# Two two-layer transformer blocks on one core: layers unrolled, weights packed as contiguous slabs, and the modulation matrices sent through the weight ring

## The chip, the cores and the metric

The kernel runs on one NeuronCore of a Trainium2 chip (trn2). The metric is the device time of one execution in microseconds (us); lower is better. Everything is float32.

## What is computed

The input x has 512 tokens of width 1024. It passes through two blocks of two layers each. A layer has a token mixer and a feed-forward part, and both are modulated by vectors that come from one conditioning vector c and a 1024 x 6144 matrix of the layer:

```
mod = silu(c) @ w_mod[l] + b_mod[l]                  # 6144 values, cut in six: sh1, sc1, g1, sh2, sc2, g2
h = _rms(x, ln1[l]) * (1 + sc1) + sh1
x = x + g1 * _mixing(h, ...)                         # w_in, three kinds of attention, w_o
h = _rms(x, ln2[l]) * (1 + sc2) + sh2
x = x + g2 * ((silu(h @ w_gate[l]) * (h @ w_up[l])) @ w_down[l])      # hidden width 2816
```

The second block has the same frame with its own matrices: its mixer has two kinds of attention and a state-space part, and its feed-forward part is `square(relu(h @ w_up)) @ w_down` with hidden width 4096. So there are four modulation matrices of 24 MB each (w_mod for two layers, w_ada_2 for two), which are used for one row only. The mod vector of a layer is needed when that layer starts.

## The kernel before

Activations lie transposed: xT and hT hold 1024 features as 8 tiles of 128 partitions x 512 tokens. Every large product takes 128 x 128 weights as the stationary operand and 512 tokens as the moving one, eight or more in a row into one bank (`gemm`, L775). One such float32 product is recorded as two MATMUL instructions, so "x32" in a row is 16 products.

Weights come in slabs of up to 2 MB (4096 words per partition) through a ring of two slots (`RING = 2`). SyncE issues the loads in a list's order (`SLABS1`, `SLABS2`, L607 and L664): slab n goes to slot n mod 2, and before its load SyncE waits until the last product that reads slab n-2 is done (`LAST1`, `LAST2`). In the feed-forward part of block 1 a slab `gu` holds two column tiles of w_gate and two of w_up and serves the steps gu 2s and 2s+1, 32 products; a slab `down` holds one column tile of w_down, 22 products. In block 2 a slab `up` serves four steps of 8 products, a slab `down` one step of 32.

The modulation matrices do not use the ring. They come as 24 pieces of 1 MB (256 columns each) into two stages that lie in the tiles SPT and sel. VectorE multiplies the eight row tiles of a piece by silu(c) and adds them (`mod_sum`, L1432 and L1434), and TensorE sums the result over the partitions with two products with a single moving column (`mod_product`, L783). For the first layer all 24 pieces are done before anything else (L588 to L596). For each following layer they are spread over the feed-forward part of the layer before (steps `ma` and `mm`), with loads issued behind the slabs. Block 2 runs its two layers as a loop over one program, so its second layer does this work as well, though no layer follows.

Each block is a hardware loop (`Fori`) over its two layers. The engines run hand-written lists of steps (`order1`, `order2`) in order; TensorE, ScalarE and VectorE each take their part of each step. A step takes banks of PSUM in turn from one of two groups of four, MAIN and SIDE. In the attention of block 1 there are 48 units (sc, nr, tp, pv), each with small products at L877, L883 and L893.

Small vectors (biases, gains, lambda) come from 40 or so small transfers issued by GpSimd; c and c_2 come from SyncE, one word per partition.

Of the kernel before, what the change touches and what calls it, by code (L numbers as in the profile page):

```python
# [42 lines left out]
RENEW = 100  # L43
# [55 lines left out]
def fresh(engine, value):  # L99

    r = engine.alloc_register()
    engine.reg_mov(r, value)
    return engine.snap(r, donate=True, min_val=0, max_val=DEPTH - 1)

class Signal:
# [8 lines left out]

    def after(self, l, k):
        return self.sem, l * self.per + (self.base + k)

    def check(self):
        assert self.seen == self.per, (self.sem, self.seen, self.per)  # L120
# [16 lines left out]
class Banks:  # L137

    def __init__(self, full, free, base):  # L140
        self.full, self.free, self.base = full, free, list(base)
        self.where, self.uses, self.turn = {}, [0] * 8, {}
# [8 lines left out]
    def bank(self, job):  # L151
        return self.where[job][0]

    def before(self, l, job):
        b, n = self.where[job]
        return self.free[b], l * self.uses[b] + (self.base[b] + n)

    def ready(self, l, job):
        b, n = self.where[job]
        return self.full[b], l * self.uses[b] + (self.base[b] + n + 1)  # L160

    def taken(self, l, job):

        b, n = self.where[job]
        return self.free[b], l * self.uses[b] + (self.base[b] + n + 1)

    def taken_before_second(self, l, job):
        b, n = self.where[job]
        return self.free[b], l * (n + 1) + self.base[b]

    def ready_before_second(self, l, job):

        b, n = self.where[job]
        return self.full[b], l * (n + 1) + self.base[b]

    def after_layers(self):
        return [self.base[b] + DEPTH * self.uses[b] for b in range(8)]
# [24 lines left out]
def order1():  # L202
    o = [("prep",), ("norm", 0)]
# [41 lines left out]
    for u in range(n + 3):  # L245
        if u < n:
            o.append(("sc", u))
        if 0 <= u - 1 < n:
            o.append(("nr", u - 1))
        if 0 <= u - 2 < n:  # L250
            o.append(("tp", u - 2))
        if 0 <= u - 3 < n:
            o.append(("pv", u - 3))
    for t in range(8 + 1):
# [5 lines left out]
    o.append(("norm", 1))  # L260
# [12 lines left out]
STEPS1 = order1()  # L273

SLABS1 = ([("qi", 0, 5), ("v", 0, 4), ("qaqb", 0, 2), ("kbkc", 0, 5), ("qc", 0, 1)]
          + [("wo", s, 1) for s in range(2)] + [("gu", s, 2) for s in range(FT1 // 2)] + [("down", s, 1) for s in range(KT)])
assert len(SLABS1) % RING == 0 and DEPTH == 2

# [4 lines left out]
LAST1.update({("down", s): ("down", s) for s in range(KT)})  # L283

def plan_banks(steps, jobs_of, full, free, base):
    b = Banks(full, free, base)
    for st in steps:
        for job, group in jobs_of(st):
            b.add(job, group)  # L290
    return b

def jobs1(st):
# [5 lines left out]
    if kind in ("norm", "pss", "rope", "idx", "bz", "br", "sc", "tp", "on"):  # L300
        return [(st, SIDE)]
    if st == ("mm", 0):
        return [(("mod",), SIDE)]
# [7 lines left out]
V2_N = W_LAM + 128  # L311

# [13 lines left out]
def order2():  # L326
    o = [("prep",), ("norm", 0)]
# [29 lines left out]
    for w, last in ((0, "wo"), (1, "down")):  # L357
# [6 lines left out]
        if w == 0:  # L364
            o.append(("norm", 1))
# [9 lines left out]
STEPS2 = order2()  # L375
SLABS2 = ([("cq", 0, 1), ("v", 0, 2), ("mix", 0, 3), ("xbc", 0, 1), ("z", 0, 1),
                                                ("aqk", 0, 1)]
          + [("wo", s, 1) for s in range(2)] + [("up", s, 1) for s in range(FT2 // 4)]
          + [("down", s, 1) for s in range(KT)])
assert len(SLABS2) % RING == 0  # L380
# [4 lines left out]
LAST2.update({("down", s): ("down", s) for s in range(KT)})  # L385

def jobs2(st):
# [9 lines left out]
    if st == ("mm", 0):  # L398
        return [(("mod",), SIDE)]
    if kind in ("norm", "cqss", "kvss", "kr", "mqr", "dtt", "tp", "an", "xd", "G", "da", "sn"):  # L400
        return [(st, SIDE)]
# [3 lines left out]
def pieces_behind(slabs, first, each):  # L405

    out, p = {}, 0
    names = [k[:2] for k in slabs]
    for n in range(names.index((first, 0)) + 1, len(names)):
        out[names[n]] = list(range(p, min(p + each, PIECES)))  # L410
        p = min(p + each, PIECES)
    assert p == PIECES
    return out

BEHIND1 = pieces_behind(SLABS1, "gu", 2)
BEHIND2 = pieces_behind(SLABS2, "up", 3)

class Slabs:  # L420

    def __init__(self, slabs, landed, base):
        self.slabs, self.landed, self.base = slabs, landed, list(base)
        self.per = [0] * RING
        self.at = {}
        for n, (kind, s, dmas) in enumerate(slabs):
            self.per[n % RING] += 16 * dmas
            self.at[(kind, s)] = (n, n % RING, self.per[n % RING])

    def slot(self, key):
        return self.at[key][1]

    def ready(self, l, key):
        n, slot, count = self.at[key]
        return self.landed[slot], l * self.per[slot] + (self.base[slot] + count)

    def after_layers(self):
        return [self.base[s] + DEPTH * self.per[s] for s in range(RING)]

def build(nc, A, out, blocks=(1, 2)):
    ctx = ExitStack()
    with ctx:
# [3 lines left out]
        def sem(name):  # L448
# [19 lines left out]
        modN = sb("modN", [P, 6 * KT])  # L468
        modT = sb("modT", [P, 6 * KT])
        bias4 = sb("bias4", [P, LAYERS, 6 * KT])  # L470
        biasN = sb("biasN", [P, 6 * KT])
        cN = sb("cN", [P, KT])
# [3 lines left out]
        cT = sb("cT", [P, 2, KT])  # L476
        csc = sb("csc", [P, 2, KT])
        vec = sb("vec", [P, V2_N])
        vall2 = sb("vall2", [P, DEPTH, V2_N])
        vall1 = sb("vall1", [P, DEPTH, 36])  # L480
# [10 lines left out]
        stage = [SPT[:, 0:4, :].rearrange("p (k a) n -> p k (a n)", k=1).rearrange("p o (k n) -> p (o k) n", k=KT),  # L491
                 sel[:, :, :].rearrange("p (k a) n -> p k (a n)", k=1).rearrange("p o (k n) -> p (o k) n", k=KT)]
        acc = [SPT[:, 4, 0:PIECE], SPT[:, 5, 0:PIECE]]
# [18 lines left out]
        cst_in = sem("cst_in")  # L512
# [21 lines left out]
        macc = sem("mod_summed")  # L534
        mread = sem("mod_read")
        mland = [sem("mod_landed0"), sem("mod_landed1")]
        mod_in = sem("mod_bias_in")
        ma1, ma2 = Signal(macc, PIECES, PIECES), Signal(macc, PIECES, PIECES * (1 + (DEPTH if 1 in blocks else 0)))
        mr1 = Signal(mread, PIECES - 1, PIECES - 1)
        mr2 = Signal(mread, PIECES - 1, (PIECES - 1) * (1 + (DEPTH if 1 in blocks else 0)))  # L540
        ml1 = [Signal(s, 8 * PIECES, 8 * PIECES) for s in mland]
        ml2 = [Signal(s, 8 * PIECES, 8 * PIECES * (1 + (DEPTH if 1 in blocks else 0))) for s in mland]
        base0 = [2] + [1] * 7
        bk1 = plan_banks(STEPS1, jobs1, full, free, base0)
        sl1 = Slabs(SLABS1, landed, [0] * RING)
        block = ctx.enter_context(nc.Block())
        do1, do2 = 1 in blocks, 2 in blocks
        base1 = bk1.after_layers() if do1 else base0
        bk2 = plan_banks(STEPS2, jobs2, full, free, base1)
        sl2 = Slabs(SLABS2, landed, sl1.after_layers() if do1 else [0] * RING)  # L550
# [12 lines left out]
        final = bk2.after_layers() if do2 else base1  # L563
# [6 lines left out]
        V_LN1, V_LN2, V_QNA, V_KNA, V_QNC, V_KNC, V_SINK, V_GOUT, V1_N = 0, 8, 16, 17, 18, 19, 20, 28, 36  # L570
        vec_in = sem("vec_in")
        vec2_in, pos_in = sem("vec2_in"), sem("pos_in")
        VEC_DMAS2 = DEPTH * 14
        VEC_DMAS1 = DEPTH * (3 + 8 + 1)
# [3 lines left out]
        def _(sp):  # L578
            sp.dma_start(cst[:, :], A["consts"]).then_inc(cst_in, 16)
# [3 lines left out]
            with nc.allow_non_contiguous_dma(reason="c lies one word per partition"):  # L583
                sp.dma_start(cT[:, 0, :], A["c"][0].rearrange("(t p) -> p t", p=P)).then_inc(x_in, 16)
                sp.dma_start(cT[:, 1, :], A["c_2"][0].rearrange("(t p) -> p t", p=P)).then_inc(x_in, 16)

            def load(sl, l, n, dst, src):
# [1316 lines left out]
```

## Time and profile before

| | |
|---|---|
| median of 3 runs | 3943.94 us (3939.78 to 3944.48) |
| span of the profiled execution | 3928.9 us |
| TensorE busy | 3512.1 us, 89% of the span, in 8996 instructions |
| VectorE busy | 1441.1 us, 37% |
| ScalarE busy | 644.8 us, 16% |
| bytes moved | 329.77 MB, mean 84 GB/s |

The profile is one execution. Its span runs from the first to the last instruction, 15 us less than the median of the timed runs. A line such as L775 is the place in the kernel's text that issued the instruction.
### The profile page before, as it was taken

To read this page: it belongs to the slowest core of one execution; us is meant where nothing else is said; L and a number is where in the kernel's file an instruction comes from. 1 tells how busy PE (TensorE), PEld (TensorE's weight loads), DVE (VectorE), ACT (ScalarE), POOL (GpSimd) and SP (SyncE) were. 2 spreads that over 40 slices of the span, in tenths; PEclk is the share of its full clock that TensorE was granted. 3 is DMA by queue.
4 is the path that set the end of the run, shared out by engine and by line. 5 is a ranking of instruction groups with operands and counts; after the bars stand their busy time and mean duration, and the time that the engine had idled before them with its cause. 6 is when DMAs were issued, how large, how long until landed. Compare 5 with 4: busy or idle time off the path is not lost.

```text
span 3928.9 us, 27849 instructions
## 1 busy us (share of the span) xinstructions
PE 3512.1 (89%) x8996; PEld 1631.5 (42%) x8996; DVE 1441.1 (37%) x3459; ACT 644.8 (16%) x1425; POOL 45.5 (1%) x61
## 2 busy tenths in 40 slices
PE   1497889999999698999997997999997998899997
PEld 1243444444444353444443443444443444344443
DVE  4548651333116854233201365344101337144101
ACT  0112441000011333100002242200001133200000
POOL 4000000000000000000000000000000000000000
PEclk6698659999999756999998977999998978999999
DMA  8621002544332000344421200255231210145331
GB/s 167 179 65 43 1 1 64 164 136 148 84 77 65 22 1 1 107 145 155 130 74 46 86 22 0 78 186 172 78 77 38 82 43 1 64 161 171 99 83 43
DMA packets 363107, 329.77 MB, mean 84 GB/s; under 512 B 31265, under 2 KB 328737, under 8 KB 362833
## 3 DMA queue, kind: packets, MB, share of 16 engines
q1 hardware_dynamic: 360656, 327.48, 27.4%
q0 software_dynamic: 2304, 0.43, 0.5%
q8 instruction: 80, 1.31, 0.1%
q14 instruction: 67, 0.54, 0.1%
HBM read 325.79 MB, written 2.10 MB: 83 GB/s over the span
## 4 chain that ended last, share of the span: by engine, by line
PE 77%; DVE 12%; DMA 6%; issue 2%; ACT 2%; SPq 1%; DVEq 0%; ACTq 0%
PE bank L775 60%; DMA sel<-in_w_mods 5%; PE bank L877 3%; PE bank L893 2%; DVE SPT L1434 2%; DMA SPT<-in_w_mods 2%; PE bank L883 1%; DVE SPT L1825 1%; PE bank L1044 1%; PE bank L858 1%; DVE sel L1535 1%; PE bank L1028 1%; PE bank L783 1%; PE bank L812 1%; DVE m L1534 1%
## 5 line engine op out<-in xcount | busy, mean ns | idle before, releaser
L775 PE MATMUL bank<-hT,ring 128*128 128x512 f32 x4032 | 1785.6, 601 | 46.7 <-DVE hT L1457 15.5
L775 PEld LDWEIGHTS bank<-hT,ring 128*128 128x128 f32 x4032 | 764.8, 192 | 994.2 <-issue 984.6
L775 PE MATMUL bank<-U,ring 128*128 128x512 f32 (+1 forms) x1760 | 760.3, 593 | 3.3 <-DVE U L1861 2.3
L775 PEld LDWEIGHTS bank<-U,ring 128*128 128x128 f32 (+1 forms) x1760 | 332.6, 190 | 421.3 <-issue 421.3
L783 PE MATMUL bank<-cst,SPT 128*128 128x1 f32 x480 | 74.3, 259 | 135.4 <-DVE SPT L1434 135.4
L1625 DVE TENSOR_TENSOR U<-U,bank 128x512 f32<-128x512 f32 x44 | 30.3, 688 | 426.6 <-PE bank L775 426.6
L1854 DVE SCALAR_TENSOR_TENSOR hT<-hT,modG,rb 128x512 f32<-128x512 f32 x16 | 11.9, 746 | 456.7 <-ACT rb L1273 456.7
L1618 DVE SCALAR_TENSOR_TENSOR xT<-bank,modT,xT 128x512 f32<-128x512 f32 x32 | 24.0, 750 | 376.5 <-PE bank L775 376.5
L783 PEld LDWEIGHTS bank<-cst,SPT 128*128 128x128 f32 x480 | 79.5, 218 | 188.4 <-DVE SPT L1434 142.2
L1434 DVE SCALAR_TENSOR_TENSOR SPT<-sel,c,SPT 128x256 f32<-128x256 f32 x252 | 122.2, 485 | 9.0
L1434 DVE SCALAR_TENSOR_TENSOR SPT<-SPT,c 128x256 f32<-128x256 f32 x252 | 122.2, 485 | 9.0
L1861 DVE TENSOR_TENSOR U<-U 128x512 f32<-128x512 f32 x64 | 44.2, 691 | 208.7 <-ACT U L1406 208.7
L1239 ACT ACTIVATE U<-bank 128x512 f32<-128x512 f32 x44 | 26.3, 597 | 575.1 <-PE bank L775 575.1
L1265 ACT ACTIVATE sqb<-bank 128x512 f32<-128x512 f32 x38 | 22.7, 597 | 581.7 <-PE bank L775 568.4
L877 PE MATMUL bank<-U 64*128 64x256 f32 (+3 forms) x192 | 112.9, 694 | 0.0
L1406 ACT ACTIVATE U<-bank 128x512 f32<-128x512 f32 x64 | 38.2, 597 | 446.8 <-PE bank L775 446.8
L893 PE MATMUL bank<-SPT,VT 128*64 128x128 f32 x384 | 101.0, 414 | 0.0
L1434 DVE SCALAR_TENSOR_TENSOR SPT<-sel,cN,SPT 128x256 f32<-128x256 f32 x168 | 81.5, 485 | 6.0
L1434 DVE SCALAR_TENSOR_TENSOR SPT<-SPT,cN 128x256 f32<-128x256 f32 x168 | 81.5, 485 | 6.0
L1148 ACT ACTIVATE hT<-xT 128x512 f32<-128x512 f32 x32 | 17.8, 619 | 395.0 <-DVE xT L1618 152.9
L947 PE MATMUL bank<-hT,cst 128*128 128x512 f32 x64 | 39.9, 774 | 43.3 <-ACT hT L1294 43.3
L775 PE MATMUL bank<-ring,hT 128*128 128x452 f32 (+1 forms) x256 | 77.9, 465 | 0.0
(237 smaller groups left out, 2731.9 us busy)
## 6 DMA issues: line engine op xcount, KB each, us to landing
SPT<-in_w_mods SPq DMA_DIRECT2D x60, 1024.0 KB, 10.0
sel<-in_w_mods SPq DMA_DIRECT2D x60, 1024.0 KB, 9.7
ring<-in_w_up SPq DMA_DIRECT2D x16, 2048.0 KB, 8.1
ring<-in_w_down SPq DMA_DIRECT2D x16, 2048.0 KB, 9.1
ring<-in_w_gate SPq DMA_DIRECT2D x22, 1024.0 KB, 5.4
ring<-in_w_up SPq DMA_DIRECT2D x22, 1024.0 KB, 7.9
ring<-in_w_down SPq DMA_DIRECT2D x16, 1408.0 KB, 7.0
ring<-in_w_in SPq DMA_DIRECT2D x8, 2048.0 KB, 7.8
```

The lines of the kernel that those rows point to most:

```text
L775: mm = pe.matmul(dst, lhs(k), rhs(k), start=(k == 0), stop=(k == n - 1))
L783: mm = pe.matmul(bank[b][:, c:c + 1], acc[p % 2][:, P * j:P * j + P], ones[:, 0:1], start=True, stop=True)
L812: mm = pe.matmul(dst[:, :], ones, hT[:, k, :], start=(k == 0), stop=(k == KT - 1))
L858: mm = pe.matmul(dst[:, P * j:SEQ], w, SP[:, h % 2, j, P * j:SEQ], start=(j == kt), stop=(j == QT - 1))
L877: pe.matmul(dst[:, 0:P * len(ks)], PT[p, q, P * i:P * i + P], PT[p, k, P * ks[0]:P * ks[-1] + P], start=True, stop=True).then_inc(*done)
L883: mm = pe.transpose(dst[:, P * j:P * j + P], S[:, u % 3, P * j:P * j + P], ident)
L893: mm = pe.matmul(dst[p, 0:P], VT[:, kb, v:v + HD], pT[:, u % 3, P * j:P * j + P], start=(j == 0), stop=(j == len(ks) - 1))
L947: mm = pe.matmul(dst[:, :], ones, hT[:, k, :], start=(k == 0), stop=(k == KT - 1))
L1028: pe.matmul(bank[b][:, 0:n], U[p, A_Q + h // 2, P * i:P * i + P], U[p, A_K + h // 2, 0:n], start=True, stop=True, tile_position=(r, 0)).th ...
L1044: mm = pe.matmul(dst[p, 0:P], VT[:, j, v:v + HD], pT[:, u % 3, P * j:P * j + P], start=(j == 0), stop=(j == i))
L1434: ins = dve.scalar_tensor_tensor(a, w[:, k, :], c[:, k:k + 1], a, ALU.mult, ALU.add)
L1861: dve.tensor_tensor(U[:, f, :], U[:, f, :], U[:, f, :], ALU.mult).then_inc(*s2["u"].up())
```

## The change

The layers are unrolled: the loops `Fori` go, each layer has its own list of steps, and waits are on constants. All weights, the modulation matrices too, are packed on the host into one array of slabs, each laid out as the ring wants it (per partition one contiguous run of up to 16 KB), and each slab is one transfer. The order of the loads is the order in which the steps first use the slabs, over all layers and kinds (`ALL_SLABS`); `RING` stays 2. Small vectors are packed into one array as well, and the constants come in two transfers.

The modulation work changes its form. A matrix is 12 slabs of 2 MB (512 columns). TensorE multiplies a slab with silu(c) as the stationary operand: `cz` holds it as 32 columns of which one is not zero, and the eight row tiles of the slab are moving operands of 512 columns, sent to four column tiles of the array in turn (`mod_gemv`, tile position 0, 32, 64 or 96). ScalarE copies the bank to sqb, and four products with one moving column sum it and turn it into columns (`mod_turn`). VectorE adds the bias. The steps are mg and mp (mg2 and mp2 for the matrix of the next layer).

For the first layer only slabs 0 to 3 (shift and scale of the mixer, 2048 values) are done at the start; slabs 4 to 11 are done inside its attention, one in five units. The matrix of the next layer is done in the feed-forward part: in block 1 slab s right behind step gu 2s+1 (the last one behind down 0), in the first layer of block 2 slab p right behind step up 2p+1. The last layer of block 2 has none. The step norm is split into ns (squares, sum, product with the root) and nh (scale and shift).

```diff
-RENEW = 100
+MOD_SLABS = 6 * D // 512
+MOD_FIRST = 4
...
-def order1():
-    o = [("prep",), ("norm", 0)]
+def order1(l):
+    if l == 0:
+        o = [("ns", 0), ("mg", 0)]
+        for s in range(1, MOD_FIRST):
+            o += [("mg", s), ("mp", s - 1)]
+        o += [("mp", MOD_FIRST - 1), ("prep",), ("nh", 0)]
+    else:
+        o = [("prep",), ("ns", 0), ("nh", 0)]
...
+        if l == 0 and u % 5 == 0 and MOD_FIRST + u // 5 < MOD_SLABS:
+            o.append(("mg", MOD_FIRST + u // 5))
+        if l == 0 and u % 5 == 3 and MOD_FIRST + u // 5 < MOD_SLABS:
+            o.append(("mp", MOD_FIRST + u // 5))
...
     for f in range(FT1):
-        o += [("gu", f), ("ma", f)] + ([("mm", f - 1)] if f else [])
+        o.append(("gu", f))
+        if f % 2 and f // 2 < MOD_SLABS:
+            o += [("mg2", f // 2)] + ([("mp2", f // 2 - 1)] if f > 1 else [])
     for n in range(KT):
         o.append(("down", n))
-        if n < 2:
-            o += [("ma", FT1 + n), ("mm", FT1 + n - 1)]
-        if n == 2:
-            o += [("mm", PIECES - 1), ("mb",)]
+        if n == 0:
+            o += [("mg2", FT1 // 2), ("mp2", FT1 // 2 - 1)]
+        if n == 1:
+            o.append(("mp2", MOD_SLABS - 1))
...
             for f in range(FT2):
                 o.append(("up", f))
-                if f % 4 < 3:
-                    p = 3 * (f // 4) + f % 4
-                    o += [("ma", p)] + ([("mm", p - 1)] if p else [])
-            o += [("mm", PIECES - 1), ("mb",)]
+                if f % 2 and l < DEPTH - 1 and f // 2 <= MOD_SLABS:
+                    p = f // 2
+                    o += ([("mg2", p)] if p < MOD_SLABS else []) + ([("mp2", p - 1)] if p else [])
...
+for _blk, _layers, _of in ((1, STEPS1, slab_of1), (2, STEPS2, slab_of2)):
+    for _l, _steps in enumerate(_layers):
+        for _st in _steps:
+            _key = _of(_st)
+            if _key is not None and (_blk, _l) + _key not in ALL_SLABS:
+                ALL_SLABS.append((_blk, _l) + _key)
...
+            sp.dma_start(small[:, :], A["small"]).then_inc(small_in, 16)
+            sp.dma_start(cst[:, 0:2 * P], A["consts"][:, 0:2 * P]).then_inc(ident_in, 16)
...
+            for n, (blk, l, kind, s) in enumerate(ALL_SLABS):
+                if n >= RING:
+                    b0, l0, k0, s0 = ALL_SLABS[n - RING]
+                    sp.wait_ge(*(bk1 if b0 == 1 else bk2).ready(l0, (LAST1 if b0 == 1 else LAST2)[(k0, s0)]))
+                w = WIDTHS[(blk, kind)]
+                sp.dma_start(ring[:, n % RING, 0:w], A["slabs"][n, :, 0:w]).then_inc(landed[n % RING], 16)
+                if n == RING - 1:
+                    sp.dma_start(cst[:, 2 * P:C_N], A["consts"][:, 2 * P:C_N]).then_inc(cst_in, 16)
...
+            def mod_gemv(dst, m, key, sl):
+
+                pe.wait_ge(*sl.ready(l, key))
+                w8 = ring[:, sl.slot(l, key), :].rearrange("p (k n) -> p k n", k=KT)
+                for k in range(KT):
+                    r = 32 * (k % 4)
+                    mm = pe.matmul(dst[r:r + 32, :], cz[:, m, k, :], w8[:, k, :], start=(k < 4), stop=(k >= 4),
+                                   tile_position=(0, r))
+                return mm
...
+            def mod_turn(dst, s):
+
+                for j in range(4):
+                    mm = pe.matmul(dst[:, j:j + 1], sqb[:, s % 2, P * j:P * j + P], ones[:, 0:1], start=True, stop=True)
+                return mm
+
+            pe.wait_ge(cz_ready, 1)
+            pe.wait_ge(cst_in, 16)
...
+                    elif kind == "mg2":
+                        s = st[1]
+                        act.wait_ge(*bk1.ready(l, st))
+                        if s >= 2:
+                            act.wait_ge(*bk1.ready(l, ("mp2", s - 2)))
+                        act.activation(sqb[:, s % 2, :], src[:, :], ACT.Copy).then_inc(mod_row2, 1)
+                        act.wait_ge(mod_row2, MOD_SLABS * l + s + 1)
+                        act.sem_inc(*freed)
```

## Rows read from the trace of the kernel before

**Rows 1.** The page: busy time of each engine.

```profile
PE 3512.1 (89%) x8996; PEld 1631.5 (42%) x8996; DVE 1441.1 (37%) x3459; ACT 644.8 (16%) x1425; POOL 45.5 (1%) x61
```

**Rows 2.** Windows by stage: length, busy of PE, PEld, DVE, ACT, POOL, granted clock, DMA share, GB/s.

```profile
0.00:166.00 166.00, 29.58 (x128) 27.34 (x128) 98.52 (x208) 3.46 (x5) 45.51 (x61) 0.60 0.79 193
410.00:559.80 149.80, 142.54 (x422) 76.76 (x422) 81.12 (x350) 54.97 (x193) 0.00 (x0) 0.58 0.00 1
659.70:973.50 313.80, 313.31 (x788) 143.74 (x788) 95.25 (x197) 21.75 (x32) 0.00 (x0) 0.99 0.43 135
973.50:1126.00 152.50, 152.47 (x364) 68.33 (x365) 16.24 (x32) 4.41 (x7) 0.00 (x0) 1.00 0.36 94
2522.60:2772.70 250.10, 237.46 (x608) 109.58 (x608) 113.25 (x231) 23.93 (x39) 0.00 (x0) 0.98 0.46 151
3429.00:3674.70 245.70, 233.64 (x608) 107.80 (x606) 112.78 (x230) 23.39 (x39) 0.00 (x0) 0.99 0.47 154
```

**Rows 3.** Timeline of SyncE (SPq) and TensorE around one gu slab's end.

```profile
717.67 0.37 SPq L588 DMA_DIRECT2D ring<-in_w_gate  x1
...
703.45 13.98 PE L775 MATMUL bank<-hT,ring 128*128 128x512 f32 x32
717.63 13.98 PE L775 MATMUL bank<-hT,ring 128*128 128x512 f32 x32
```

**Rows 4.** DMA issues (count, KB, median us to landing), and GB/s per us from 310.

```profile
GB/s 0 20 240 408 403 412 391 223 0 0 0 0 0 8 0 0 0 0 0 0 0 0 0 0 0 0 0 0 0 0 0 0 0 0 0 0 25 178 371 403
ring<-in_w_o SPq DMA_DIRECT2D x2, 2048.0 KB, 7.8
...
ring<-in_w_down SPq DMA_DIRECT2D x16, 1408.0 KB, 7.0
cst<-in_consts SPq DMA_DIRECT2D x1, 2248.0 KB, 10.2
```

**Rows 5.** TensorE timeline: products on 32 columns; one 64-row product; two 32-row tiles; clock.

```profile
2139.05 7.05 PE L775 MATMUL bank<-hT,ring 128*32 128x512 f32 x16
...
474.30 1.22 PE L877 MATMUL bank<-U 64*128 64x256 f32 x2
...
2289.13 1.22 PE L1028 MATMUL bank<-U 32*128 32x256 f32 x4
...
470.00:480.00 10.00, 10.00 (x31) 5.41 (x31) 5.79 (x27) 3.90 (x16) 0.00 (x0) 0.50 0.01 2
2285.00:2295.00 10.00, 8.90 (x32) 4.04 (x28) 8.14 (x36) 4.16 (x18) 0.00 (x0) 0.50 0.00 0
```

**Rows 6.** TensorE timeline around short pauses (in brackets the idle time and its releaser).

```profile
2689.88 0.61 PE L783 MATMUL bank<-cst,SPT 128*128 128x1 f32 x4 [2.56 <-DVE SPT L1434]
2690.34 8.81 PE L775 MATMUL bank<-hT,ring 128*128 128x512 f32 x16
...
2713.53 7.11 PE L775 MATMUL bank<-hT,ring 128*128 128x512 f32 x16
...
2753.95 10.02 PE L775 MATMUL bank<-hT,ring 128*128 128x512 f32 x16
```

**Rows 7.** Windows of 1 us after TensorE idle times of 3.1 us, columns as in rows 2.

```profile
661.00:662.00 1.00, 1.00 (x2) 0.34 (x1) 1.00 (x3) 1.00 (x2) 0.00 (x0) 0.50 1.10 347
1137.00:1138.00 1.00, 1.00 (x4) 0.42 (x3) 1.00 (x2) 1.00 (x2) 0.00 (x0) 1.00 0.00 0
```

**Rows 8.** Timeline of the first 180 us: TensorE and ScalarE.

```profile
22.45 5.28 PE L766 MATMUL bank<-cst,U 128*128 128x128 f32 x32 [22.45 <-DMA cT<-in_c]
34.46 0.98 PE L783 MATMUL bank<-cst,SPT 128*128 128x1 f32 x4 [6.73 <-DVE SPT L1434]
166.00 8.65 PE L812 MATMUL bank<-hT,cst 128*128 128x512 f32 x16 [1.03 <-ACT hT L1148]
176.80 5.75 ACT L1157 ACTIVATE hT<-hT,modT,modA 128x512 f32<-128x512 f32 x8 [0.76 <-DVE hT L1497]
177.76 8.82 PE L775 MATMUL bank<-hT,ring 128*128 128x512 f32 x20 [3.11 <-ACT hT L1157]
```

More of the change, by code:

```diff
@@ L114, in up, with now, check @@
         return self.sem, 1
+    def now(self):
+        return self.sem, self.base + self.seen
     def after(self, l, k):
         return self.sem, l * self.per + (self.base + k)
-    def check(self):
-        assert self.seen == self.per, (self.sem, self.seen, self.per)
+    def check(self, times):
+        assert self.seen == times * self.per, (self.sem, self.seen, self.per)
 class Chain:
@@ L140, in __init__ @@
     def __init__(self, full, free, base):
-        self.full, self.free, self.base = full, free, list(base)
-        self.where, self.uses, self.turn = {}, [0] * 8, {}
+        self.full, self.free, self.uses = full, free, list(base)
+        self.where, self.turn = {}, {}
     def add(self, job, group):
@@ L283, with plan_banks @@
 LAST1.update({("down", s): ("down", s) for s in range(KT)})
-def plan_banks(steps, jobs_of, full, free, base):
+LAST1.update({("mod", s): ("mg", s) for s in range(MOD_SLABS)})
+LAST1.update({("mod2", s): ("mg2", s) for s in range(MOD_SLABS)})
+def plan_banks(layers, jobs_of, full, free, base):
     b = Banks(full, free, base)
-    for st in steps:
-        for job, group in jobs_of(st):
-            b.add(job, group)
+    for l, steps in enumerate(layers):
+        for st in steps:
+            for job, group in jobs_of(st):
+                b.add((l,) + job, group)
     return b
@@ L397, in jobs2 @@
         return [(("post", st[1]), SIDE)] if st[2] == 0 else []
-    if st == ("mm", 0):
-        return [(("mod",), SIDE)]
-    if kind in ("norm", "cqss", "kvss", "kr", "mqr", "dtt", "tp", "an", "xd", "G", "da", "sn"):
+    if kind in ("mg2", "mp2", "ns", "cqss", "kvss", "kr", "mqr", "dtt", "tp", "an", "xd", "G", "da", "sn"):
         return [(st, SIDE)]
     return []
[L405 to L413, printed above, removed]
@@ L443, in build @@
+def build(nc, A, out):
     ctx = ExitStack()
@@ L533, in build @@
         )
[L534 to L545, printed above, removed]
+        mod_row2 = sem("mod_row2")
+        bk1 = plan_banks(STEPS1, jobs1, full, free, [1] * 8)
+        sl1, sl2 = Slabs(1, landed), Slabs(2, landed)
         block = ctx.enter_context(nc.Block())
[L547 to L550, printed above, removed]
+        bk2 = plan_banks(STEPS2, jobs2, full, free, bk1.uses)
         s2 = dict(
@@ L581, in _ @@
             sp.dma_start(U[:, 0:8, :].rearrange("p (t a) n -> p t (a n)", t=QT),
                          A["x"][0].rearrange("(t p) d -> p t d", p=P)).then_inc(x_in, 16)
[L583 to L587, printed above, removed]
-                sp.dma_start(dst, src).then_inc(landed[n % RING], 16)
@@ L1105, in _ @@
-            if do2:
-                pe.wait_ge(*s2["x"].after(DEPTH - 1, 2 * KT))
-            else:
-                for n in range(KT):
-                    pe.wait_ge(*bk1.taken(DEPTH - 1, ("down", n)))
+            def mod_gemv(dst, m, key, sl):
[6 more added lines that the diff above has]
+                return mm
@@ L1452, in normed @@
                 if s1["pn"].seen:
-                    dve.wait_ge(*s1["pn"].after(l, s1["pn"].seen))
+                    dve.wait_ge(*s1["pn"].now())
                 link(dve.tensor_tensor(a, rb[:, k % 2, :], rb[:, k % 2, :], ALU.mult))
```

2379 lines of the change are left out of this document (1151 added, 1228 removed).

## The prediction

> **What bounds the kernel now.** I read the page first: TensorE is busy 89% of the span, VectorE 37% [rows 1]. The table by stage shows where that average hides two kinds of time [rows 2]. In the feed-forward stages TensorE has no holes: 313.3 of 313.8 us with the granted clock at 0.99 (gu, block 1) and 152.5 of 152.5 (down). In the first 166 us it does 29.6 us of work, while the first modulation matrix comes in and VectorE adds it up. The attention of block 1 is TensorE too, 142.5 of 149.8 us, but at a clock of 0.58.
>
> Then I looked at what the ring does when a slab is used up [rows 3]. The step pair that starts at 703.45 ends near 717.6; SyncE issues the next load at 717.67; TensorE starts the next 32 products at 717.63. It waits for nothing, since the other slot already holds the next slab. The load has a whole slab's time (28.3 us) to land. A 2 MB load lands 7.8 us after its issue and moves 390 to 412 GB/s while it runs; a down slab takes 7.0 us [rows 4].
>
> So two things decide: the 166 us at the start, which the change shortens, and the cover of the ring's loads.
>
> **The change part by part.** One product of 128 rows with 512 columns is 0.865 us (32 instructions, 13.84 of the 14.18 us from 703.45 to 717.63 [rows 3]); the other 0.34 us are the two small products of a modulation piece.
>
> *Cost of one modulation slab on TensorE.* Eight products with 32 stationary columns. Alone such a product costs what a full one does: 8 in 6.98 us [rows 5]. No row shows column tiles together. The nearest are row tiles: at a clock of 0.50 two products on different 32-row tiles (four instructions) take 1.22 us, as one 64-row product of the same 256 columns does (two instructions) [rows 5]. So disjoint tiles ran at the same time, in float32. The bounds are two rounds, 1.73 us, and no overlap, 6.9 us. I take the low end with some overhang, 2.0 us (3.8 at a clock of 0.50), because the row tiles overlapped fully. The turn (four small products) is twice a piece's: 0.7 us, or 1.9 at half clock (0.98 for two in [rows 8]).
>
> The Trainium skill speaks against this choice: "TensorE: Matmul & The Clock Gate", Part 3, says that weight loads overlap running matmuls only when the row group differs, and all four column tiles use the same rows; its measured speedup for three column tiles is 2.38. No trace of this kernel shows it. By full serialization the sum is the second rival below.
>
> *Start.* Now the first projection begins at 177.76 [rows 8]. After: the constants, which everything waits for, are the sixth transfer; 9.0 MB at 390 GB/s plus some 3 us give 26. The transposes (5.3 us) are covered by that. Squares and the sum over partitions: 1.1 + 8.65 us [rows 8], to 36. Slabs 0 and 1: to 41. SyncE can load slab 2 only when slab 0 is read (38.5), so it lands at 46.5, slab 3 near 49; with products and turns partly at half clock these end near 60. Preparation and the first scaled tile: 62. The qi slab, issued when slab 2 is read (about 50), has landed by 58. Gain 116 us. The 40 GpSimd transfers and the c loads vanish inside this.
>
> *Eight slabs in the attention of the first layer.* TensorE is the bound there, so all of it adds: 8 x (3.8 + 1.9) = 46 us at that clock [rows 2, 5]. ScalarE's copies (0.6 us each) lie beside it.
>
> *Feed-forward of block 1, two layers.* This is the large term. The list is now gu 0, mod 0, gu 1, mod 1 and so on, and the ring still has two slots: all gu slabs share one slot, all mod slabs the other. Slab gu s+1 may be loaded only when gu s is finished, exactly when TensorE wants it. What TensorE has meanwhile is one slab product and one turn, 2.7 us. The gap is the load: 0.1 + 7.8 + 0.1 = 8.0 us, ten times; then down 0 and down 1, same reason (22-product slabs, 6.1 us if their rate rises to that of 2 KB rows, 7.0 at most [rows 4]). From down 2 on the ring is doubled again. Away go 24 x 0.34 = 8.2 us. Idle for some 5 us, TensorE is likely to be slowed: after 2.56 us of idle and one small product the next eight products took 8.81 instead of 7.11 us, another time 10.02 [rows 6]; after 3.1 us the clock fell once and once not [rows 7]. I take 1.9 us for each of twelve. Sum per layer: 80 + 12.2 + 22.8 - 8.2 = 107; twice 214 us. VectorE's sums go, but it was no bound (95 of 313.8 us [rows 2]).
>
> *Up stage, first layer of block 2.* Here each up slab has two mod slabs behind it. The odd one takes the slot that the up slab leaves, and the next up slab is issued right after it: 4.2 MB at 400 GB/s, landing 7.9 and about 12.9 us after the last product. TensorE waits 7.9, multiplies cold and turns (5.7), so 13.6, plus 1.9 for the clock; the even slab adds 2.7. That is 18.2, six times: 109 us. The stage now takes 250.1 us for 32 groups of 6.92 = 222 [rows 2]; these pieces' 27 us go. Net 82.
>
> *Up stage, last layer.* No modulation work: 245.7 falls to about 225. Gain 21.
>
> *Unrolling and contiguous slabs.* The products follow each other at 0.4325 us per instruction in the loops already, so I cost the loop at nothing; in the attention of block 1, TensorE's idle 7.3 of 149.8 us [rows 2] bounds what leaner waits could gain in such a stage, and longer code fetches could cost as much. Contiguity gains nothing where 2 KB rows reach 400 GB/s [rows 4]; the constants (17.6 KB rows) took 10.2 us for 2.2 MB with other transfers in the queues. That bounds a slab at 9.3 us, and the sum at +45 for 30 exposed loads. The skill's "DMA: Bandwidth & Descriptors", Specifications, gives about 358 GB/s as a core's share of HBM; the measured 412 says otherwise, and by the page each load would be 0.7 us longer, 21 us in all.
>
> Sum: -116 + 46 + 214 + 82 - 21 = +205 on a span of 3928.9, so 4134. The median of the runs stands 15 us above the span: **4149 us**.
>
> **The rivals.** *A. Column tiles do not overlap.* Then a slab is 6.9 us (up to 13.7 at half clock). In block 1's feed-forward the load hides it (6.9 + 0.7 against 8.0), and with only 0.4 us idle the clock stays: 2 x (92.2 - 8.2) = 168. Start -98, attention about 93, up stage 6 x (7.9 + 10 + 1.2 + 7.6) - 27 = 133, last -21: +275, 4219 us.
>
> *B. The clock stays up.* No penalty after the gaps, and slabs in the attention at 2.7 us each: start -116, 22, 168, up stage 6 x (12.9 + 2.7) - 27 = 67, last -21: +120, 4064. For it speaks the second of [rows 7], against it a clock of 0.58 in the attention.
>
> *C. The loads are covered after all: faster.* If the next gu or up slab were there when the turn ends, each place would cost only the 2.7 us of TensorE: -116 + 46 + 2 x (32 - 8) + (32 - 27) - 21 = -38, 3906 us. It decides by one number: on average over the 30 places the slab must land within 1.3 us (38 / 30) after the turn, or 4.0 us after the last product of the slab before. At 7.8 us per load this needs twice the rate seen, or a third slot. The change text has two.
>
> *D. The matrices gain nothing at the start,* because constants and four slabs come late: proj at 100 instead of 62. Then 4187, inside the range.
>
> **How the numbers follow.** Forecast 0.55, A 0.20, B 0.13, D 0.06, C 0.05, rest 0.01. The range holds B at 4064 and A at 4219, with a little outside for a load of 7.3 or 9.3 us: 4050 to 4235. A measurement of this kernel can tell 0.2%, 8 us, from no change. Faster 0.05 (C), same 0.01, slower 0.94.
>
> **What would show each step.** In the trace after: projections begin near 62 us; mg2 groups of 16 instructions take about 2 us (A: 7); before each gu and down 0 and 1 TensorE waits 5 us for the DMA of the ring, 20 + 4 times, and twice per up slab in the first layer of block 2; SyncE issues a gu load at the end of the slab before and it lands 7.8 us later; the granted clock is 0.50 behind these waits; the last up stage takes 225 us. The forecast is wrong if the waits before gu are under 2 us (C), or if TensorE's own time for the slabs is three times mine (A).

## The result, and the profile after

The changed kernel takes 4077.27 us (median of 4 runs, 4059.55 to 4083.53) against 3941.86 us for the kernel before (4 runs, 3937.27 to 3944.48). The ratio is 1.034, 95% interval 1.032 to 1.037: slower, as forecast, inside the range, and 72 us below the predicted 4149. The profiled execution of after has a span of 4078.3 us, 149.4 more than that of before.

The page of after answers [rows 1 and 4]. In order: busy time of each engine, packets, the chain that ended last (shares by engine), the three groups that wait for the ring (L622 is `gemm`, L631 `mod_gemv`; busy, mean ns, idle before and its releaser), and the loads with their time to landing.

```profile
PE 3630.3 (89%) x9668; PEld 1645.8 (40%) x9668; DVE 999.9 (25%) x2538; ACT 673.9 (17%) x1473; POOL 1.7 (0%) x6
...
DMA packets 22952, 304.37 MB, mean 75 GB/s; under 512 B 2464, under 2 KB 2592, under 8 KB 3760
...
PE 81%; DVE 8%; DMA 7%; issue 3%; ACT 2%; DVEq 0%; SPq 0%; ACTq 0%
...
L622 PE MATMUL bank<-hT,ring 128*128 128x512 f32 x4032 | 1817.0, 612 | 150.8 <-DMA ring<-in_slabs 107.1
...
L622 PE MATMUL bank<-U,ring 128*128 128x512 f32 (+1 forms) x1760 | 768.5, 598 | 18.0 <-DMA ring<-in_slabs 15.1
...
L631 PE MATMUL bank<-ring,cz 128*32 128x512 f32 x768 | 110.8, 703 | 52.6 <-DMA ring<-in_slabs 52.6
...
ring<-in_slabs SPq DMA_DIRECT2D x124, 2048.0 KB, 7.8
ring<-in_slabs SPq DMA_DIRECT2D x16, 1408.0 KB, 6.2
```

TensorE is as busy as before in share, 89%, and does 118 us more. VectorE lost 441 us and GpSimd 44. What that work had cost TensorE before lay at the start and in short pauses of block 2's up stages (2.56 us in [rows 6]). New is the DMA of the ring in the chain: TensorE stands idle for it 107 us in front of gu slabs and the first projection, 15 us in front of down slabs and 53 us in front of modulation slabs. The packets fell from 363,107 to 22,952, and a 2 MB load lands in 7.8 us, as the loads with rows of 2 KB did before [rows 4].

The same stages as in [rows 2], in the columns of that table:

```profile
0.00:61.04 61.04, 29.60 (x145) 16.30 (x145) 12.76 (x31) 14.18 (x22) 1.71 (x6) 0.81 0.68 267
316.30:450.00 133.70, 129.78 (x566) 67.58 (x566) 68.91 (x327) 52.67 (x184) 0.00 (x0) 0.73 0.35 126
548.78:927.00 378.22, 326.64 (x874) 142.41 (x875) 18.39 (x35) 24.00 (x38) 0.00 (x0) 0.91 0.28 109
927.00:1124.61 197.61, 189.76 (x472) 84.12 (x471) 7.12 (x12) 9.36 (x13) 0.00 (x0) 0.97 0.23 84
2620.58:2943.23 322.65, 273.62 (x801) 118.45 (x801) 27.23 (x50) 31.08 (x51) 0.00 (x0) 0.90 0.33 125
3601.24:3824.37 223.13, 221.67 (x512) 97.74 (x513) 25.40 (x38) 23.91 (x39) 0.00 (x0) 0.99 0.19 67
```

The window of the attention (316.30 to 450.00) is narrower than the one in [rows 2]. From the starts of the stages in both timelines comes the balance of the span:

| stage | before | after | difference | forecast |
|---|---|---|---|---|
| start, to the first projection | 177.8 | 61.0 | -116.7 | -116 |
| block 1, layer 1: projections and attention, to w_o | 413.5 | 418.6 | +5.2 | +46 |
| block 1, layer 1: feed-forward (gu and down) | 466.4 | 575.8 | +109.5 | +107 |
| block 1, layer 2: feed-forward (gu and down) | 466.5 | 572.9 | +106.4 | +107 |
| block 2, layer 1: up | 250.1 | 322.7 | +72.5 | +82 |
| block 2, layer 2: up | 246.2 | 223.1 | -23.1 | -21 |
| all else (six pieces between -10.2 and +2.6) | | | -4.4 | 0 |
| span | 3928.9 | 4078.3 | +149.4 | +205 |

**The gu stage.** TensorE and SyncE's queue (SPq) in after, answering [rows 3]; the number in brackets is the idle time before the group.

```profile
691.74 1.92 PE L631 MATMUL bank<-ring,cz 128*32 128x512 f32 x16
691.84 39.86 SPq L592 DMA_DIRECT2D ring<-in_slabs  x4
693.60 1.05 PE L638 MATMUL bank<-cst,sqb 128*128 128x1 f32 x8
699.77 29.69 PE L622 MATMUL bank<-hT,ring 128*128 128x512 f32 x64 [5.12 <-DMA ring<-in_slabs]
```

The last product on slab gu 3 ends at 691.74, SyncE issues the load of gu 4 at 691.84, and the product that needs it starts at 699.77. Between them TensorE has one modulation slab (1.92 us) and one turn (1.05), and waits 5.12 us. Then the 64 instructions take 29.69 us, where the undisturbed stage needs 27.7: the granted clock behind the first of these waits is 0.50 for some 5 us (the window below) and then 1.00 (592 to 616). From the start of one slab's products to the start of the next it is 37.75 us (662.02 to 699.77) against 28.36 before: +9.4, where the forecast's terms give 8.0 + 1.9 - 0.7 = 9.2.

```profile
586.00:591.00 5.00, 4.90 (x6) 2.18 (x7) 0.00 (x0) 0.00 (x0) 0.00 (x0) 0.50 0.78 331
```

**The up stage** of block 2's first layer, the second and the first half of two up slabs:

```profile
2746.96 3.64 PE L631 MATMUL bank<-ring,cz 128*32 128x512 f32 x16 [7.90 <-DMA ring<-in_slabs]
2750.53 1.87 PE L638 MATMUL bank<-cst,sqb 128*128 128x1 f32 x8
2752.26 15.42 PE L622 MATMUL bank<-hT,ring 128*128 128x512 f32 x32
```

Here the modulation slab itself is late by the whole load, 7.9 us, and is then multiplied at half clock. There are six such waits, 7.7 to 8.0 us each.

**The attention of block 1.** Eight slabs were put into a stage in which TensorE hardly rests, and the stage grew by only 5 us. The windows say why: 316.3 to 450 ran at a granted clock of 0.73, while nearly the same part of it, the 48 units with their small products, had 0.52 before:

```profile
430.00:559.00 129.00, 126.12 (x361) 66.68 (x360) 68.93 (x318) 46.66 (x175) 0.00 (x0) 0.52 0.00 1
```

Around one slab, TensorE's timeline in after, and the windows over it:

```profile
339.35 1.22 PE L728 MATMUL bank<-U 64*128 64x256 f32 x2
...
341.74 3.64 PE L631 MATMUL bank<-ring,cz 128*32 128x512 f32 x16
345.31 0.71 PE L728 MATMUL bank<-U 64*128 64x256 f32 x2
...
350.28 1.05 PE L638 MATMUL bank<-cst,sqb 128*128 128x1 f32 x8
...
353.31 1.22 PE L728 MATMUL bank<-U 64*128 64x256 f32 x2
```

```profile
341.74:345.30 3.56, 3.56 (x17) 0.59 (x16) 0.65 (x2) 0.82 (x4) 0.00 (x0) 0.50 0.00 0
345.30:350.30 5.00, 4.85 (x29) 2.75 (x25) 3.59 (x18) 2.71 (x9) 0.00 (x0) 0.99 0.78 262
...
353.30:356.10 2.80, 2.80 (x9) 1.50 (x8) 1.74 (x8) 1.29 (x7) 0.00 (x0) 0.50 0.00 0
```

The score product of a unit takes 1.22 us ahead of the slab (clock 0.50), 0.71 behind it (0.99), and 1.22 again some 8 us later. By this reading the slab pays for itself with the faster units behind it. That is the theory which the experiments had to test, beside those on the feed-forward part.

The second layer of block 1 has no slabs in its attention and is a control for the unrolling. The same stretch in before and in after:

```profile
1400.00:1540.00 140.00, 132.70 (x370) 67.73 (x369) 75.08 (x296) 57.61 (x176) 0.00 (x0) 0.54 0.00 1
```

```profile
1400.00:1540.00 140.00, 133.26 (x373) 68.61 (x371) 74.24 (x300) 57.14 (x178) 0.00 (x0) 0.54 0.00 1
```

The clock is 0.54 in both, and projections plus attention take 414.0 us before and 416.5 after. So neither the unrolled program nor the contiguous slabs raised the clock or shortened this stage.

### The profile page after: what moved, and what is told of

It is laid out like the page before. It is cut to its first block, busy times and chain, and to the rows that moved or that the text cites. A ratio compares the mean times of both kernels' runs of the same rounds, so it can differ in the third digit from the quotient of the medians.

```text
span 4078.3 us, 25590 instructions
## 1 busy us (share of the span) xinstructions
PE 3630.3 (89%) x9668; PEld 1645.8 (40%) x9668; DVE 999.9 (25%) x2538; ACT 673.9 (17%) x1473; POOL 1.7 (0%) x6
## 2 busy tenths in 40 slices
DMA packets 22952, 304.37 MB, mean 75 GB/s; under 512 B 2464, under 2 KB 2592, under 8 KB 3760
## 4 chain that ended last, share of the span: by engine, by line
PE 81%; DVE 8%; DMA 7%; issue 3%; ACT 2%; DVEq 0%; SPq 0%; ACTq 0%
PE bank L622 64%; DMA ring<-in_slabs 6%; PE bank L728 2%; PE bank L744 2%; PE bank L631 1%; PE bank L734 1%; DVE SPT L1678 1%; PE bank L894 1%; PE bank L709 1%; DVE sel L1394 1%; PE bank L878 1%; PE bank L663 1%; DVE m L1393 1%; PE bank L937 1%; PE bank L885 1%
## 5 line engine op out<-in xcount | busy, mean ns | idle before, releaser
L622 PE MATMUL bank<-hT,ring 128*128 128x512 f32 x4032 | 1817.0, 612 | 150.8 <-DMA ring<-in_slabs 107.1
L622 PEld LDWEIGHTS bank<-hT,ring 128*128 128x128 f32 x4032 | 786.3, 196 | 1153.6 <-issue 1143.4
L622 PE MATMUL bank<-U,ring 128*128 128x512 f32 (+1 forms) x1760 | 768.5, 598 | 18.0 <-DMA ring<-in_slabs 15.1
L622 PEld LDWEIGHTS bank<-U,ring 128*128 128x128 f32 (+1 forms) x1760 | 336.0, 191 | 444.0 <-issue 444.0
L631 PE MATMUL bank<-ring,cz 128*32 128x512 f32 x768 | 110.8, 703 | 52.6 <-DMA ring<-in_slabs 52.6
L728 PE MATMUL bank<-U 64*128 64x256 f32 (+3 forms) x192 | 99.1, 615 | 0.0
L622 PE MATMUL bank<-ring,hT 128*128 128x452 f32 (+1 forms) x256 | 77.9, 465 | 0.0
L920 PE MATMUL bank<-SPT,sel 128*64 128x512 f32 (+3 forms) x128 | 59.0, 603 | 16.9 <-DVE SPT L1680 16.8
L1076 ACT ACTIVATE SPT<-SPT,st 128x256 f32<-128x256 f32 (+3 forms) x96 | 48.8, 508 | 146.8 <-DVE st L1446 83.8
L631 PEld LDWEIGHTS bank<-ring,cz 128*32 128x32 f32 x768 | 22.9, 121 | 120.6 <-issue 120.5
L744 PEld LDWEIGHTS bank<-SPT,VT 128*64 128x64 f32 x384 | 57.9, 189 | 24.8 <-issue 23.7
L689 PE MATMUL bank<-U,cst 128*128 128x512 f32 x48 | 29.1, 691 | 43.2 <-DVE U L1306 43.2
L638 PEld LDWEIGHTS bank<-cst,sqb 128*128 128x128 f32 x384 | 51.2, 207 | 39.0 <-issue 39.0
```

The source lines that it names most:

```text
L622: mm = pe.matmul(dst, lhs(k), rhs(k), start=(k == 0), stop=(k == n - 1))
L631: mm = pe.matmul(dst[r:r + 32, :], cz[:, m, k, :], w8[:, k, :], start=(k < 4), stop=(k >= 4), tile_position=(0, r))
L638: mm = pe.matmul(dst[:, j:j + 1], sqb[:, s % 2, P * j:P * j + P], ones[:, 0:1], start=True, stop=True)
L728: pe.matmul(dst[:, 0:P * len(ks)], PT[p, q, P * i:P * i + P], PT[p, k, P * ks[0]:P * ks[-1] + P], start=True, stop=True).then_inc(*done)
L744: mm = pe.matmul(dst[p, 0:P], VT[:, kb, v:v + HD], pT[:, u % 3, P * j:P * j + P], start=(j == 0), stop=(j == len(ks) - 1))
L920: mm = pe.matmul(dst[p, P * s:SEQ], sel[:, s, HD * h:HD * h + HD], mixing(4 * h + s)[:, P * s:SEQ], start=(s == 0), stop=(s == QT - 1))
```

## The experiments

All are edits of the changed kernel. The first four ran on one chip with the kernel before at 3932.41 us (7 runs, 3930.83 to 3950.69), the fifth with 3934.17 (9 runs, 3926.85 to 3939.69).

**1. The modulation slabs leave the ring.** The slabs of the next layer's matrix land in SPT and sel, which are idle in the feed-forward part, half in each, issued behind the weight slabs. The ring then alternates over weight slabs alone, as before the change (`RINGED` is ALL_SLABS without them). TensorE's work and all else stay.

```diff
-            for n, (blk, l, kind, s) in enumerate(ALL_SLABS):
+            for n, (blk, l, kind, s) in enumerate(RINGED):
...
+                for key in BEHIND.get((blk, l, kind, s), ()):
...
+                        sp.wait_ge(*bk.ready(l, ("mg2", key[3] - 1)))
...
+                    src = A["slabs"][ALL_SLABS.index(key)]
+                    sp.dma_start(SPT[:, 0:4, :].rearrange("p k n -> p (k n)"), src[:, 0:SLAB // 2]).then_inc(staged, 16)
+                    sp.dma_start(sel[:, :, :].rearrange("p k n -> p (k n)"), src[:, SLAB // 2:SLAB]).then_inc(staged, 16)
```

> The changed kernel with one difference: the slabs of the next layer's modulation matrix (mg2) do not pass through the weight ring but land in SPT and sel, half a slab in each, which lie idle in the feed-forward stage; products, column tiles and turns are the same. Theory 1 (the ring's loads lost their cover): the waits before gu, down 0, down 1 and up vanish, each place costs only TensorE's own 2.9 us; gu and down of block 1 take 466 - 8 + 12 x 2.9 = 492 us instead of 576 per layer, the up stage of block 2's first layer 257 instead of 323, the whole 4077 - 168 - 66 = 3843 us. Theory 2 (the modulation work on TensorE, switching to column tiles and back, and the falling clock cost the time): the same products in the same places cost the same, and the time stays above 4000 us.

Measured: 3834.66 us (3822.19 to 3841.32), ratio to before 0.974, interval 0.972 to 0.976; a span of 3839.4. That is 239 us less in the span than the changed kernel (taken on another chip, where the kernel before was 9 us slower), and 98 us faster than the kernel before on its own chip. TensorE and SPq of this kernel (L650 is `gemm`, L664 `mod_gemv`, L610 the ring's load):

```profile
577.97 0.33 SPq L610 DMA_DIRECT2D ring<-in_slabs  x1
578.75 1.04 PE L664 MATMUL bank<-sel,cz 128*32 128x512 f32 x8
579.72 27.73 PE L650 MATMUL bank<-hT,ring 128*128 128x512 f32 x64
579.85 0.33 SPq L621 DMA_DIRECT2D SPT<-in_slabs  x1
...
607.49 0.33 SPq L610 DMA_DIRECT2D ring<-in_slabs  x1
```

No wait stands in brackets, the 64 instructions take 27.73 us, and each load is issued a whole slab's time before its use. The two half slabs land in 8.4 and 10.5 us instead of 7.8 and no product waits for them. So the loss of the change is the way the modulation slabs share the ring's two slots, some 240 us made up of waits and of the clock behind them; without it the change is a gain of 98 us. The same order with a third slot, which would separate the order from the number of slots, was not run.

**2. More work in the wait.** In block 1 each slab of the next matrix is multiplied three times (the repeats write the same numbers again).

```diff
-                for k in range(KT):
+                for k in [k for _ in range(3 if sl is sl1 and key[0] == "mod2" else 1) for k in range(KT)]:
```

> The changed kernel, but in block 1's feed-forward each modulation slab is multiplied three times into the same bank (8 products become 24), 3.7 us more work for TensorE in each of 24 places; the result is the same. Theory 1: the work lies in the wait for the ring's load and costs nothing in itself. If the falling clock is due to the 5 us of idle time, it stays at full speed now and each slab after a wait takes 27.8 instead of 29.7 us: 4077 - 22 x 1.9 = 4035 us; if the clock falls all the same, 4077. Theory 2 (TensorE's own work costs): 4077 + 24 x 3.7 = 4166 us.

Measured: 4071.93 us (4070.59 to 4076.61), ratio to before 1.036, interval 1.034 to 1.037, where the changed kernel had 1.034 (1.032 to 1.037). 24 slabs x 3.4 us = 83 us of added TensorE work cost nothing that can be measured. Its timeline in the gu stage and at down 1 (977.52), and then two windows behind the wait that ends at 618.39:

```profile
609.85 5.36 PE L631 MATMUL bank<-ring,cz 128*32 128x512 f32 x48
...
618.39 29.40 PE L622 MATMUL bank<-hT,ring 128*128 128x512 f32 x64 [2.20 <-DMA ring<-in_slabs]
...
977.52 19.12 PE L622 MATMUL bank<-U,ring 128*128 128x512 f32 x44
```

```profile
618.00:624.00 6.00, 5.61 (x9) 2.41 (x10) 0.00 (x0) 0.00 (x0) 0.00 (x0) 0.72 0.67 281
624.00:630.00 6.00, 6.00 (x15) 2.66 (x14) 0.00 (x0) 0.60 (x1) 0.00 (x0) 1.00 0.00 0
```

The wait shrank from 5.1 us to 2.2 us here and to between 1.5 and 1.6 us from 732.02 on, about by the 3.4 us that were added: the time of the place is set by the load, not by TensorE. I had expected that so short a wait might leave the clock up, and gave 4035 us for that. It did not: 2.2 us of idle still cost 1.7 us of clock (29.40 against 27.73), and so did five of the six waits near 1.6 us. Only at down 0 and down 1, where the added work fills the wait entirely, does the group behind run at full rate, 19.13 and 19.12 us instead of 21.43 and 20.82.

**3. One column tile.** All eight products of a slab go to the same 32 columns of the array, one after another.

```diff
-                    r = 32 * (k % 4)
-                    mm = pe.matmul(dst[r:r + 32, :], cz[:, m, k, :], w8[:, k, :], start=(k < 4), stop=(k >= 4),
-                                   tile_position=(0, r))
+                    mm = pe.matmul(dst[0:32, :], cz[:, m, k, :], w8[:, k, :], start=(k == 0), stop=(k == KT - 1),
+                                   tile_position=(0, 0))
...
-                    mm = pe.matmul(dst[:, j:j + 1], sqb[:, s % 2, P * j:P * j + P], ones[:, 0:1], start=True, stop=True)
+                    mm = pe.matmul(dst[:, j:j + 1], sqb[0:32, s % 2, P * j:P * j + P], ones[0:32, 0:1], start=True, stop=True)
```

> The changed kernel with all eight products of a modulation slab on one column tile, so that none can overlap; the turn sums 32 partitions. A slab takes 6.9 us instead of 1.9 if the speed came from four tiles at once, and still 1.9 if it did not. Theory 1: in block 1's feed-forward 6.9 + 1.0 us fit in the wait of 8.0, the stage does not grow and, with no idle time, the clock stays up: 576 falls to about 555 per layer; start, attention and the up stage of block 2 grow by some 10, 40 and 80 us: 4077 - 42 + 130 = 4165 us. Theory 2: every place grows by 5 us, 4077 + 44 x 5 = 4297 us or more.

Measured: 4154.82 us (2 runs, 4153.25 and 4156.38), ratio to before 1.056, interval 1.054 to 1.058. A slab and the group behind it in its gu stage (L630 is `mod_gemv` there):

```profile
625.02 7.05 PE L630 MATMUL bank<-ring,cz 128*32 128x512 f32 x16
633.00 27.70 PE L622 MATMUL bank<-hT,ring 128*128 128x512 f32 x64 [0.93 <-DMA ring<-in_slabs]
```

A slab takes 7.05 us on one tile and 1.92 on four: in float32 the four column tiles do run together, 3.7 times as fast. This rejects the forecast's rival A as an account of the changed kernel, and is what rival A looks like when it is made to happen; it came out 64 us below its 4219, mostly in the attention of the first layer, which took 456.7 us, 43 more than in before, where A had put 93. In the gu stage the slower slab costs little, since it fills the load's time: with 0.93 us of idle the next group takes 27.70 us, so the clock stays up. The Trainium skill has two rules that bear on this: "TensorE: Matmul & The Clock Gate", Part 3, lets weight loads overlap only when the row group differs (its table still has a speedup of 2.38 for three column tiles), while "TensorEngine Tiling (Array Packing)", Tiling Modes, says that different tiles load weights and multiply in parallel, and counts 4 tiles for 32 columns. The four tiles here share their rows, and 3.7 agrees with the second page.

**4. All twelve slabs at the start.** The first layer's matrix is finished before its attention.

```diff
-MOD_FIRST = 4
+MOD_FIRST = 12
```

> The changed kernel with all twelve slabs of the first modulation matrix at the start (MOD_FIRST = 12), none in the attention of the first layer. The start grows by eight slabs, bound by the ring's two slots at about 6.5 us each: +52 us. Clock theory (the dense slab products raise the granted clock in the attention, from 0.52 to 0.73, and so pay for themselves): the attention gets no shorter than 3 us, 4077 + 49 = 4126 us, and its clock falls back to 0.52. Rival (the slabs cost their 35 us of TensorE time there, and the unrolled waits had made the attention 30 us leaner): 4077 + 52 - 35 = 4094 us.

Measured: 4125.78 us (4121.56 to 4127.68), ratio to before 1.049, interval 1.047 to 1.050. The start grows from 61.0 to 109.2 us, by 48.2. Projections and attention of the first layer take 414.4 us (109.19 to 523.58) instead of 418.6. So the eight slabs cost about 4 us where they stood. The second half of this kernel's attention:

```profile
370.00:500.00 130.00, 127.09 (x371) 67.61 (x370) 64.62 (x294) 47.74 (x166) 0.00 (x0) 0.53 0.00 1
```

Without the slabs the clock is 0.53 again, as in before. The removal alone does this.

**5. Slabs put into an attention that had none.** As experiment 1, but ten of the twelve slabs which the second layer of block 1 multiplies for block 2 move from its gu stage into its attention, one in five units, through the ring, which is idle there.

```diff
+        if l == 1 and u % 5 == 0 and u // 5 < 10:
+            o.append(("mg2", u // 5))
+        if l == 1 and u % 5 == 3 and u // 5 < 10:
+            o.append(("mp2", u // 5))
...
+        if l == 1:
+            if f in (1, 3):
+                o.append(("mg2", 10 + f // 2))
...
```

> Edit: as in e_staged, but ten of the twelve modulation slabs that block 1's second layer multiplies for block 2 move from its gu stage into its attention, one in five units, through the ring (which is idle there). Theory 1, the dense slab products raise the granted clock of the attention by what they cost, as in the first layer: the attention grows by about 6 us (10 x 0.65), the gu stage loses 10 x 2.7 = 27 us, total 3834.7 - 21 = 3814 us, and the attention's granted clock rises from about 0.54 to about 0.73. Rival, what was seen in the first layer was an accident of that place: ten slabs cost 10 x (3.6 + 1.9) = 55 us less the 27, total 3863 us, and the clock stays near 0.54 between them.

Measured: 3808.63 us (5 runs, 3807.86 to 3823.82), ratio to before 0.969, interval 0.967 to 0.971: the fastest of all, below experiment 1 and 3.1% below the kernel before. Projections and attention of that layer as one window, first in experiment 1, then here:

```profile
1049.05:1462.26 413.21, 357.93 (x931) 173.89 (x931) 246.23 (x685) 132.21 (x335) 0.00 (x0) 0.75 0.07 26
```

```profile
1044.88:1452.17 407.29, 349.44 (x1170) 167.49 (x1171) 246.53 (x695) 138.39 (x345) 0.00 (x0) 0.85 0.22 78
```

With ten slabs more to multiply the stage is 5.9 us shorter, and TensorE is busy 8.5 us less in 239 more instructions. In the second half the clock is 0.85 (1310 to 1440) instead of 0.54 (1314 to 1444). TensorE's timeline there:

```profile
1350.59 1.92 PE L676 MATMUL bank<-ring,cz 128*32 128x512 f32 x16
1352.45 0.70 PE L773 MATMUL bank<-U 64*128 64x256 f32 x2
```

Slab and unit both run at full clock. The rival, that the first layer was an accident of its place, expected 3863 us and a clock near 0.54, and falls. Theory 1 had put +6 us for the stage, and it was -5.9. One execution does not fix the sign: the first layer's stage, the same program in the changed kernel, in experiment 1 and here, took 418.6, 418.5 and 414.7 us. And the medians of experiments 1 and 5 differ by 26.0 us, of which the ten slabs that leave the gu stage at 2.8 us each account for 28. What is clear of that is that 38 us of slabs and turns (26.2 + 12.2) cost about nothing.

The clock of the whole window was higher than in the first layer (0.85 against 0.73) mainly because more units have a slab. Here the ten slabs reach to the end. In the first layer the last of the eight is turned at 411.64, and the units behind it fall back to half clock. The changed kernel from its third slab on, and then behind its last one; then experiment 5 from its third slab to its last turn:

```profile
341.70:414.66 72.96, 71.43 (x366) 36.71 (x365) 41.84 (x204) 32.28 (x117) 0.00 (x0) 0.85 0.47 173
414.66:449.27 34.61, 34.61 (x102) 18.34 (x101) 13.80 (x52) 10.10 (x28) 0.00 (x0) 0.52 0.00 0
```

```profile
1323.58:1420.28 96.70, 94.64 (x502) 48.51 (x501) 55.06 (x256) 43.55 (x145) 0.00 (x0) 0.89 0.48 175
```

What of a slab raises the clock, its products, the turn or the load that follows it, no run separates. A load alone does not do it: from 586 to 591 the DMA share was 0.78 and the clock 0.50. That the dense products do it is my reading.

## Why the prediction was right, and where its sizes were off

**The bound and the mechanism: right.** The change puts a modulation slab between every two weight slabs of a ring of two slots, so a weight slab's load starts only when the product that needs it could. Forecast 107 us per feed-forward part of block 1; measured 109.5 and 106.4. Experiment 1 takes the modulation slabs of the next layer out of the ring and gets the time back; experiment 2 shows that the load's end sets the start of each group, whatever TensorE does meanwhile.

**The single terms.** Load 8.0 us: 7.93 (691.84 to 699.77). Down 0 and 1 6.1 each: the 1408 KB loads landed in 6.2, but the first layer's gaps were 7.2 (954.73 to 961.95) and 6.5 us (983.31 to 989.76). Slab product 2.0 us: 1.92; at half clock 3.8: 3.64. Turn 0.7 us: 1.05, hidden in the wait. Clock penalty 1.9 us: 29.7 - 27.7 = 2.0. That penalty came from pauses of 2.56 us in [rows 6], and experiment 2 confirms it for 2.2 us.

**The start: -116 forecast, -116.7 measured, in part by luck.** The first projection began at 61.04, forecast 62. The wait for slab 2 was the predicted one (48.40 starts after 5.07 us), but the end of the chain was not: the last turn was done at 57.07 instead of 60, and the projection then waited 3.97 us for its own slab, which the forecast had landed by 58. The two errors cancel:

```profile
38.71 3.64 PE L631 MATMUL bank<-ring,cz 128*32 128x512 f32 x32
...
48.40 3.60 PE L631 MATMUL bank<-ring,cz 128*32 128x512 f32 x16 [5.07 <-DMA ring<-in_slabs]
...
61.04 3.75 PE L622 MATMUL bank<-hT,ring 128*128 128x512 f32 x4 [3.97 <-DMA ring<-in_slabs]
```

**The term that was mis-sized: the eight slabs in the attention, +46 forecast, +5.2 measured.** The step "TensorE is the bound there, so all of it adds" took the clock of the stage as given. The slabs changed that clock, for themselves and for everything behind them. They took 32 us themselves (22.1 for the eight slabs, 10.0 for the turns) and not 46, since most of them ran partly or wholly at full clock; and the stage around them became some 27 us shorter. I had a row for the clock, 0.58, and asked only what it does to the slabs, not what the slabs do to it. Experiments 4 and 5 show it from both sides. This is 41 of the 56 us by which the span's sum was too high.

**The up stage: 82 forecast, 72.5 measured.** The six waits of 7.9 us are as forecast. (The last part of the prediction names two waits per up slab, its sum counts one, and the trace has one.) From one up slab to the next it takes 15.4 and 17.3 us in turn more than the 27.96 us of its two undisturbed groups (2681.68, 2725.08 and 2770.38 are such starts), mean 16.4, against my 18.2: in every second one the turn ran mostly at full clock (1.18 us at 2707.10 instead of 1.87) and the group behind took 13.97 instead of 15.42, so that the clock's penalty fell away. TensorE shows no further wait ahead of these groups, so the later landing of the next up slab hid behind slab and turn, as in the sum. A little is arithmetic: 250.1 - 222 is 28, where the sum took off 27.

**What is left of the difference.** Pieces in which I had put 0 gave -4.4 us. The largest are -10.2 between the last down of block 1 and the up stage of block 2, and +2.6 in the projections and attention of block 1's second layer; no run here says of what. And 16 us are the step from span to median: for before they stood 15 us apart, for after the median is 1 us below the span. That offset belonged to one execution and did not carry over; the difference of the medians, 135 us, is therefore smaller than that of the spans.

**The rivals.** A (which one sentence of the prediction calls the second) fell: a slab took 1.92 us, and experiment 3 shows what A looks like. B (4064) lies nearest in its number, 13 us below the measured time, but its reason does not hold in the feed-forward parts, where the clock fell behind every wait for a gu slab. Its term for the attention (22 us) went the right way, though not far enough, and its 67 us for the up stage lie nearer to the measured 72.5 than my 82, since the penalty did fall away at every second up slab. C fell: the loads took 7.8 us where it needed 4.0. D fell: the first projection began at 61 us, not at 100.

**Contiguity.** It brought nothing to a 2 MB load whose rows had been 2 KB (7.8 us in [rows 4] and 7.8 after), and the bound of 9.3 us from the constants was not approached. Where the rows had been 512 bytes, the packing did shorten the load, as the forecast had it for the down slabs of block 1: 2 MB of w_down_2 landed in 9.1 us before (below) and in 7.8 after, 1408 KB of w_down in 7.0 and 6.2. TensorE waits for none of these loads, but for down 0 and 1 of block 1 after the change.

```profile
ring<-in_w_down SPq DMA_DIRECT2D x16, 2048.0 KB, 9.1
```

## What to carry to other kernels

A ring's depth is counted in loads between the release of a slot and the use of what is put into it: a second stream interleaved one to one turns two slots into one for each stream, and costs a whole load per slab and the clock behind it (9.4 us in 37.8 here). So give the second stream its own landing place, or put its slabs where the first stream has none: both together turned a kernel 3.4% slower into one 3.1% faster. Before an addition to a stage that runs at a low granted clock is priced, ask what it does to the clock: slabs put between small products cost about nothing twice here.

## What the runs showed of the hardware that I had not expected

- A modulation slab raises the granted clock of the small products behind it. The attention of block 1, in which TensorE is hardly idle even without slabs (127.1 of 130 us in experiment 4), ran at 0.52 to 0.54 without them and, from the third slab on, at 0.85 and 0.89 where there was one slab of 16 matmul instructions in five units.
- In the gu stage the clock's penalty hardly depends on the length of the pause: 1.7 us behind 2.20 us and 2.0 behind 5.12, none behind 0.93 (27.70 us). It isn't certain either: in experiment 2 a pause of 1.55 us cost 1.7 us (29.40, at 806.47) and one of 1.54 us nothing (27.70, at 918.27), and the pause of 3.1 us ahead of block 1's second gu stage cost 1.7 us in experiment 5 (29.40 for the 64 instructions) and nothing in experiment 1 (27.70).
- Four column tiles with 128 rows and 512 float32 columns ran 3.7 times as fast as one (1.92 and 7.05 us for eight products).
- A 2 MB load lands in 7.8 us with rows of 2 KB and with rows of 16 KB, but in 9.1 us with rows of 512 bytes.
